# Split merge-gate products, probabilities turned one step later and paired roots in a two-layer attention, recurrence and expert kernel

## The reference

```
(sh1, sc1, g1, sh2, sc2, g2) = silu(cond) @ w_ada + b_ada         # two conditions: context, latent
h = rmsnorm(x) * (1 + sc1) + sh1
q, k, v, xr, gr, ga, gb = split(h @ w_in)                         # gr, ga, gb: 1024 columns each
att = softmax(q k / sqrt(128), with a sink) v                      # 8 heads x 3 blocks of 128 queries
xc  = conv4(xr)
for d in (forward, backward):                                      # 8 channel blocks of 128 each
    r, i = sigmoid(blockdiag(xc) + b)                              # two gates
    log_a = -8 * r * softplus(-lambda);  a = exp(log_a)
    h = a * h + sqrt(1 - a^2) * (i * xc)                           # a scan over time
rnn = sum of both directions
merged = sigmoid(ga) * (att @ w_ap) + sigmoid(gb) * ((gelu(gr) * rnn) @ w_rp)
x = x + g1 * (merged @ w_out)
x = x + g2 * experts(rmsnorm(x) * (1 + sc2) + sh2)                 # 16 experts, top 2
```

## Time and profile before

| | |
|---|---|
| median of 3 runs | 1539.71 us (1538.92 to 1546.27) |
| the profiled execution | 1542.47 us, of which the span is 1540.7 us |
| mean granted TensorE clock | 0.992 of full speed |
| busy share of the span | PE 97%, PEld 78%, DVE 72%, ACT 60%, POOL 12% |
| gate steps of layer 0 | 204 to 333 us |
| gate steps of layer 1 | 953 to 1081 us |
| experts | about 480 to 775 us and 1223 to 1517 us |

### The profile page before, as it was taken

One profiled execution on the slowest core, in us unless ns is written; L12 is line 12 of the kernel. 1 busy time (PEld: TensorE's weight loads), 2 busy tenths in 40 slices (PEclk: granted clock), 3 DMA queues, 4 the chain that ended last, 5 costly groups with the idle time before them and its releaser, 6 DMA issues.

```text
span 1540.7 us, 19726 instructions
## 1 busy us (share of the span) xinstructions
PE 1490.0 (97%) x7489; PEld 1197.9 (78%) x7489; DVE 1108.2 (72%) x1719; ACT 922.4 (60%) x1178; POOL 181.7 (12%) x220
## 2 busy tenths in 40 slices
PE   6999999999999999999999999999999999999996
PEld 4699876669986888888768998666899678888885
DVE  4447656674647999999864665767564689999986
ACT  1323569981225877778752245899422478778774
POOL 0100012210121000000230000222004111000002
PEclk8999999999999999999999999999999999999999
DMA  9455432216539999999854554111431899999993
GB/s 353 168 188 202 163 115 82 99 59 216 203 144 340 362 401 408 410 406 409 311 186 174 187 196 165 63 64 62 163 111 55 312 358 408 413 411 408 405 354 124
DMA packets 132421, 371.98 MB, mean 241 GB/s; under 512 B 9184, under 2 KB 12640, under 8 KB 132320
## 3 DMA queue, kind: packets, MB, share of 16 engines
q1 hardware_dynamic: 113728, 326.57, 56.4%
q0 software_dynamic: 10144, 24.13, 4.5%
q10 hardware_dynamic: 8448, 19.94, 3.3%
HBM read 350.66 MB, written 19.94 MB: 241 GB/s over the span
## 4 chain that ended last, share of the span: by engine, by line
PE 86%; DVE 6%; ACT 4%; DMA 2%; issue 2%; SPq 0%; DVEq 0%; ACTq 0%
PE bank L561 24%; PE bank L917 23%; PE bank L923 12%; PE bank L550 10%; PE bank L571 3%; PE bank L768 2%; DMA ring<-in_w_ada 2%; PE bank L889 2%; PE bank L741 1%; PE bank L596 1%; PE bank L580 1%; PE bank L678 1%; PE bank L673 1%; PE bank L960 1%; PE bank L1025 1%
## 5 line engine op out<-in xcount | busy, mean ns | idle before, releaser
L1977 DVE TENSOR_TENSOR spot_low<-spot,piece_high 128x2048 fp32r<-128x2048 f32 x192 | 433.6, 2286 | 33.2 <-ACT piece_high L1336 32.0
L1336 ACT ACTIVATE piece_high<-spot 128x2048 fp32r<-128x2048 f32 x192 | 366.7, 1917 | 44.5 <-PE bank L923 42.4
L917 PE MATMUL bank<-piece_high,ga_r 128*128 128x512 f32 x768 | 308.7, 402 | 2.9 <-DVE spot_low L1977 1.6
L917 PE MATMUL bank<-spot_low,ga_r 128*128 128x512 f32 x768 | 301.7, 393 | 0.0
L923 PE MATMUL bank<-piece_high,ga_r 128*128 128x512 f32 x768 | 210.9, 396 | 3.3 <-DVE ga_r L1983 3.3
L561 PE MATMUL bank<-parts_r,ga_r 128*128 128x384 f32 x768 | 202.6, 345 | 0.0
L550 PE MATMUL bank<-hT,ring 128*128 128x384 f32 x544 | 184.7, 494 | 4.1 <-ACT ga L1274 2.3
L923 PEld LDWEIGHTS bank<-piece_high,ga_r 128*128 128x128 f32 x768 | 144.0, 188 | 38.6 <-DVE ga_r L1983 4.4
L917 PEld LDWEIGHTS bank<-piece_high,ga_r 128*128 128x128 f32 x768 | 144.3, 188 | 36.1 <-DVE spot_low L1977 2.4
L917 PEld LDWEIGHTS bank<-spot_low,ga_r 128*128 128x128 f32 x768 | 144.6, 188 | 30.6
L550 PEld LDWEIGHTS bank<-hT,ring 128*128 128x128 f32 x544 | 102.0, 192 | 70.8 <-issue 3.6
(11 more groups left out here) (336 smaller groups left out, 2333.3 us busy)
## 6 DMA issues: line engine op xcount, KB each, us to landing
spot<-in_w_gate_up SPq DMA_DIRECT2D x128, 1024.0 KB, 8.0
spot<-in_w_down SPq DMA_DIRECT2D x64, 1024.0 KB, 8.0
ring<-in_w_ada SPq DMA_DIRECT2D x24, 2048.0 KB, 9.0
ring<-in_w_in SPq DMA_DIRECT2D x22, 2048.0 KB, 7.9
expert_rows<-gb ACTq DMA_DIRECT2D x28, 512.0 KB, 7.0
ring<-in_w_attn_proj SPq DMA_DIRECT2D x4, 2048.0 KB, 8.1
ring<-in_w_rnn_proj SPq DMA_DIRECT2D x4, 2048.0 KB, 12.4
ring<-in_w_out SPq DMA_DIRECT2D x4, 2048.0 KB, 8.6
```

What stands on the lines that cost most here:

```text
L917: pe.matmul(out[n], high[:, 2 * q + k, :], w[:, k, n * 512:(n + 1) * 512], start=(q == 0 and k == 0 and i == 0), stop=False)
L1336: ac.activation(highs[p % HIGHS], spots[u], ACT.Copy).then_inc(S("piece_high"), 1)
L1977: ve.tensor_tensor(spots_low[u], spots[u], highs[p % HIGHS].bitcast(F32), ALU.subtract)\
```

## The change

1. ga and gb become split products. Their high parts (16 per layer) are made by POOL, in its queue between the gate-weight DMAs; their low parts by DVE. High parts lie in the buffers G0 to G2 (tile gb), spare, and X0, X1 (tile xc, once the scans of pairs 0 to 5, or 0 to 11, have ended).
2. `probs_turned(i - 1)` stands after `scores(i)` and ahead of product i, where `probs_turned(i)` stood after it; `pt_copy` and `att_copy` follow by a step, `pt` has one buffer instead of two.
3. The recurrent temporaries have three sets. `scan` follows two steps after its pair's gates. The square goes: where sqrt(1 - a^2) was the root of (1 + a^2) * tanh(x), with a = exp(-x), it is now (1 + a) times the root of tanh(x/2). So the root comes first, straight from `lru_tables`, and DVE multiplies after it.
4. `lru_root` runs for two pairs in even steps, instead of one in each.
5. The rnn tiles are split in high and low during the ap products (`rnn_split`), pairs 14 and 15 are scanned there, the split attention output and merged go to hT and qT instead of parts.
6. `mod_sum` turns the four 128x128 blocks with transposes, and DVE adds the four groups out of PSUM with one reduction and adds the bias in a second operation.

The diff, cut to its core:

```diff
-SPLIT = [(kind, n) for kind in ("q", "xr", "gr", "ap", "rp", "wo") for n in range(KT)]
+SPLIT = [(kind, n) for kind in ("q", "xr", "gr", "ga", "gb", "ap", "rp", "wo") for n in range(KT)]
+LATE = 5 * KT
+HIGH_HOMES = (["G0", "G1", "G2"] * 2 + ["G0", "G1"]
+              + ["G2", "spare", "X0", "G2", "spare", "X0", "spare", "X1"]
+              + ["X0", "spare", "X1"] + (["A0", "A1", "A2", "spare"] * KT)[:3 * KT - 3])
+SCANS_OF_HOME = {"X0": 6, "X1": 12}
...
                 for j in range(4):
-                    mm = pe.matmul(bank[:, 2 * j:2 * j + 2], ada_part(cc)[:, j * P:(j + 1) * P], sumsel,
-                                   start=(j == 0), stop=(j == 3), skip_group_check=True)
+                    mm = pe.transpose(bank[:, j * P:(j + 1) * P], ada_part(cc)[:, j * P:(j + 1) * P], ident)
...
                     scores(i)
-                    if kind == "gr":
-                        split_product(l, kind, i, parts_r[:, 0], parts_r[:, 1])
-                    else:
-                        product((l, kind, i % KT), s, i % 4, h_all)
+                    if i >= 1:
+                        probs_turned(i - 1)
+                    split_product(l, kind, i % KT, parts_r[:, 0], parts_r[:, 1])
                     if i % 4 == 0 and i <= KT:
                         mod_sum(l, 7 + i // 4)
-                    probs_turned(i)
...
                     ac.activation(th, a, ACT.Tanh, bias=c_log[1], scale=c_log[1])
-                    link(ac.activation(a, a, ACT.Exp, bias=c_log[0], scale=c_log[0]))
-                    if m:
-                        ac.wait_ge(S("lru_square"), m)
-                    ac.activation(a2, a, ACT.Square).then_inc(S("lru_act"), 1)
+                    ac.activation(a, a, ACT.Exp, bias=c_log[0], scale=c_log[0]).then_inc(S("lru_act"), 1)
...
                 for i in range(3 * KT):
+                    if i > KT:
+                        lru_tables(i - KT - 1)
                     exps(i)
-                    if i > KT:
-                        lru_root(i - KT - 1)
+                    if i >= 1:
+                        pt_copy(i - 1)
+                    if i >= 2:
+                        att_copy(i - 2)
+                    if i > KT and i % 2 == 0:
+                        lru_root(i - KT - 2)
+                        lru_root(i - KT - 1)
...
-                ve.tensor_tensor(modT[:, cc * 4:cc * 4 + 4, 0], pair[:, :, 0], b, ALU.add)
-                ve.tensor_tensor(modT[:, cc * 4:cc * 4 + 4, 1], pair[:, :, 1], b, ALU.add)\
+                link(ve.tensor_reduce(m, groups, AX.X, ALU.add))
+                ve.tensor_tensor(m, m, b.rearrange("p (j a) -> p j a", a=1).broadcast_to([P, 4, 2]), ALU.add)\
...
+                def scan_inputs(n):
+                    ve.wait_ge(S("lru_act"), m + 1)
+                    ve.scalar_tensor_tensor(ti, ti, 1.0, xc[:, j, :], ALU.add, ALU.mult)
+                    ve.wait_ge(S("root_ready"), m + 1)
+                    link(ve.scalar_tensor_tensor(th, a, 1.0, th, ALU.add, ALU.mult))
+                    link(ve.tensor_tensor(th, th, ti, ALU.mult))
...
                     softmax_max(i)
+                    if i > KT + 1 and i % 2:
+                        scan_inputs(i - KT - 2)
+                    if i >= KT and i % 2 == 0:
+                        low_part(2 * KT + i + 1)
                     softmax_norm(i)
...
-                    if i > KT:
-                        one_minus_square(i - KT - 1)
-                        scan(i - KT - 1)
+                    if i >= KT - 1 and i % 2:
+                        low_part(2 * KT + i + 1)
+                    if i > KT + 1:
+                        if i % 2 == 0:
+                            scan_inputs(i - KT - 2)
+                        scan(i - KT - 2)
...
                 for n in range(KT):
-                    low_part(EARLY + n + AHEAD)
+                    low_part(LATE + n + AHEAD)
+                    if n < 2:
+                        scan_inputs(14 + n)
+                        scan(14 + n)
+                    for j in RNN_SPLIT_AT.get(n, ()):
+                        rnn_split(j)
...
+                def high_part(at):
+                    kind, n = SPLIT[at]
+                    s, use, _ = CHUNK_SLOT[CHUNK_AT[(l, f"{kind}{n // 4}")]]
+                    po.wait_ge(S(f"w_loaded{s}"), 16 * (use + 1))
+                    if home_user_ahead(at):
+                        po.wait_ge(S("gemm_done"), G_AT[(l, *SPLIT[home_user_ahead(at)])] + 1)
+                    elif HIGH_HOMES[at - EARLY] in SCANS_OF_HOME:
+                        po.wait_ge(S("lru_used"), l * 16 + SCANS_OF_HOME[HIGH_HOMES[at - EARLY]])
+                    else:
+                        po.wait_ge(S("gemm_done"), G_AT[(l, *SPLIT[at - PAIRS_OF_PARTS])] + 1)
+                    po.tensor_copy(w_high_part(kind, n), slot_kn(s)[:, :, n % 4 * P:(n % 4 + 1) * P])\
+                        .then_inc(S("w_high_p"), 1)
+                for n in range(2):
+                    gate_weights(n)
+                    high_part(EARLY + n)
+                for n in range(2 * KT - 2):
+                    if n:
+                        gate_weights(n + 1)
+                    high_part(EARLY + 2 + n)
+                gate_weights(15)
```

More of the change, by code:

```diff
@@ L113, with home_user_ahead @@
 PAIRS_OF_PARTS = 3
-LATE_HIGHS = 4
+LATE = 5 * KT
[3 more added lines that the diff above has]
+SCANS_OF_HOME = {"X0": 6, "X1": 12}
+def home_user_ahead(at):
+    same = [b for b in range(EARLY, at) if HIGH_HOMES[b - EARLY] == HIGH_HOMES[at - EARLY]]
+    return same[-1] if same else None
 UNITS = [(h, b) for h in range(HEADS) for b in range(3)]
+RNN_SPLIT_AT = {2: (0,), 3: (1, 2), 4: (3,), 5: (4, 5), 6: (6,), 7: (7,)}
 PAIRS = [(d, j) for j in range(KT) for d in range(2)]
@@ L307, in build @@
         w_parts = [(part(gaf_r, i), part(gbf_r, i)) for i in range(PAIRS_OF_PARTS)]
-        late_high = [part(spare_r, 0)] + [part(hTf, i) for i in range(LATE_HIGHS - 1)]
+        high_home = {"spare": part(spare_r, 0)}
+        for i in range(3):
+            high_home[f"G{i}"], high_home[f"A{i}"] = part(gbf_r, i), part(flat_parts_r, i)
+        for i in range(2):
+            high_home[f"X{i}"] = part(xcf, i)
         ring_r = sb_r("ring")
@@ L771, in _ @@
                         attend(i - 1)
+                probs_turned(3 * KT - 1)
                 modulation(l, 10)
@@ L1289, in scaled @@
                         .then_inc(S("router_a"), 1)
-                for at in range(EARLY, len(SPLIT)):
-                    if at + AHEAD < len(SPLIT):
+                for at in range(LATE, len(SPLIT)):
+                    if LATE < at < len(SPLIT) - AHEAD:
                         high_part(at + AHEAD)
@@ L1666, in _ @@
                         mod_add(l, 4)
+                if l:
+                    link(ve.memset(xp[:, 2 + CTX:2 + LAT0], 0.0))
                 for j in range(KT):
```

116 lines of the change are left out of this document (57 added, 59 removed).

## The result

| | median us | lowest to highest | runs |
|---|---|---|---|
| before | 1540.90 | 1538.92 to 1546.27 | 4 |
| changed | 1523.41 | 1520.51 to 1526.79 | 4 |

The ratio is 0.9879, with an interval of 0.9854 to 0.9904: 17.5 us faster, where 31 were forecast. The profiled execution took 1526.79 us with a span of 1524.8; it is the slowest of the four and 3.4 us above their median.

A forecast was written before the change was run, and what follows sets the result against it. PE bounded the kernel, and DVE would bound the changed gate steps. Gates -21, gr -2, mod_sums -7 and tail -1 sum to -31 us: 1542.47 to 1511.5 profiled, 1509 as median; range 1488 to 1545.

The forecast's parts named there:

- port rival: Gate steps: a cast of about 1.05 us wholly on DVE's path, full step 8.1 us; 1522 to 1546 us, chance 0.23.
- my own sign: Gate steps: PE idle before split products or scores ended by DVE confirms DVE as bound; ended by ACT's tanh, uneven roots.
- The sign for the port: Gate steps: DVE's low part at 1.22 us would refute the port cost, at 1.5 or more confirm it.
- The products and the sum without the port: Gate steps: split products 4.23 us instead of 5.16; DVE's 6.75 plus root wait 0.3, before the port's 0.3.
- port term: Gate steps: POOL's cast holds up DVE operations with two SBUF inputs, 0.54 x 0.6 = 0.3 us per step.
- "whole cast" rival: Gate steps: a 1.05 us cast wholly on DVE's path; step 8.1 us, about 1528 to 1532; span 1522 to 1546, chance 0.23.
- slower rival: Full gate steps: POOL wins the port with a slow cast, 2.4 us per step; about 1569 us, chance 0.10.
- gr term: gr steps: transposes of the probabilities turned one step later get a product more of cover; -1 us per layer, -2.
- The mod_sum: Modulation sums by transposes: 0.5 us less each, 16 of 24 on PE's path; -7 us taken.
- The root's wait: Even gate steps: DVE waits 0.6 us for ACT's root, 0.3 per step; bounds 0 and 0.9 per even step.
- The tail: Between the loop and ap: of PE's 1.0 us idle, -0.5 us per layer, -1 in all.
- The rnn splits and scans in ap: ap products: some 30 us of DVE beside 34 of PE costs nothing; without cover, 2 to 4 us per layer.

The follow-up runs named there:

- e3: Against the changed kernel: ACT takes the two roots of even gate steps ahead of the exponentials instead of behind them; 1526.3 us.
- e1: Against the changed kernel: POOL writes zeros into the high parts of ga and gb instead of casting weights, so it reads nothing; 1508.3 us.
- e5: Against the changed kernel: the 16 casts per layer move from POOL to ACT, two in each odd step ahead of the tanh; 1519.3 us.
- e8: e5 and e6 together: casts on ACT, and copies ahead of the exponentials; 1507.6 us.
- e2: Against the changed kernel: each POOL cast for ga and gb is done twice, one after the other; 1546.6 us.
- e7: Against the changed kernel: the modulation sums are products against the 0/1 matrix again instead of transposes and a reduction; 1531.4 us.
- e10: Against the changed kernel: one root in each step from the tenth on instead of two in every second step; 1558.0 us.
- e9: Against e8: the last merge-gate cast on ACT moves from the end of step 21 to behind the exponentials of step 22; 1502.8 us.
- e4: Against the changed kernel: ga and gb products in f32 again, without casts and low parts, right operand the high part of h alone; 1529.1 us.
- e6: Against the changed kernel: ACT copies pt and the attention output ahead of the exponentials in all 24 steps; 1513.3 us.
- e11: The edits of e1 and e6 together on the changed kernel: zeros stored instead of casts, and copies ahead of the exponentials; 1500.8 us.

## Why the prediction was right and wrong

**Right in direction and range, too high in the gain.** 1523 lies 14 us above the 1509 forecast, 1 us outside the likeliest case's own span (1500 to 1522) and just inside that of the port rival (1522 to 1546). Of the 15 us between forecast and profile, 8.6 lie in the gate steps and tail, 6.7 in the gr steps and 2.5 in the mod_sums; ap and what lies outside the layers gave 2.5 back. That the time stayed in the range with two terms this far off owes something to luck.

**The signs.** The products took 4.2 us and the table loads in the gate steps of layer 0 fell from 28 to 14, as named. PE's long idles there ended with ACT's tanh, which by my own sign "would put it on the uneven roots". e3 moved the roots and gained nothing, and e1 left the roots alone and took half of the idle away, so that sign did not tell the two apart: the tanh comes last in a chain that DVE's stretches push later. What is left of the idle in e1, 4.9 and 4.6 us with the tail's 1.4, may be the roots'; no run shows it. The sign for the port was badly chosen as well: 28 of the 32 low parts kept 1.22 us, one took 1.39 and three over 2, while most of the stretches fell on other operations.

**The products and the sum without the port: right.** The split product took 4.23 us. Without the port term my sum gives 14 x 7.05 + 2 x 6.9 + 1 = 113.5 us per layer against 128.9, which with the tail's 0.5 puts the gate stage at 133.7 - 15.9 = 117.8. With no read on POOL it was 118.5 and 118.4. One part of that sum did not come: the last cast, for which I took 1 us of wait, ran at 310.65 us and its low part at 313.31 us, with no wait on it. On ACT, in e5 and e8, the same cast did hold up the list.

**The port term was mis-sized.** I took 0.3 us per step: a stretch of 0.54 us for 60% of the casts, 8.4 us in all. The share was about right: 18 of the 32 casts met a stretched operation. The stretch itself was taken at half its size: it measured 1.0 us on average and up to 1.5. The rows I scaled from were of other POOL operations and of one collision. The stretches add up to 8 us in layer 0 and 10.8 in layer 1, and e1 puts what reaches the gate stage at 6.7 and 10.0 us, 0.52 us per cast; e2 has 0.62. That is 8 us more than I took, nearly all that is missing in the gate steps. Some 6 us of the 16.7 come through the four stretches at half clock, about 1.5 us each, a path that no term foresaw. The 1.05 us taken for the cast itself was right (1.055). My "whole cast" rival priced a step at 1.05 and came too high, since 14 of the 32 casts met no operation that they stretched. The slower rival had its threshold at 1.36 us per step; the cast kept its length beside DVE, as that rival had it, but with 1.06 us the threshold could not be reached. e2, with two casts per step, did end slower than before, by 0.3%.

**The gr term had the wrong sign.** "Turned one step later these have a whole product more of cover: -1 us per layer" looked at the transposes and left out the copy behind them on ACT, which stands behind the exponentials and their wait for DVE. The stage got 2.4 us longer per layer; with the copy moved it got 1.6 shorter than before, somewhat more than forecast.

**The mod_sum: right in kind, too large.** 0.36 us instead of 0.5 on PE's path, and of the 16 some have no share in it (rp in layer 1 did not move). The stages show 4.5 us for the forecast 7; undoing it (e7) cost 4.6 in the stages.

**The root's wait: right, slightly high.** 0.6 us per even step was forecast, 2.4 us over seven was measured in layer 0, 0.34 each. I did not see how much hung on the pairing, with DVE's list written as it is: e10 is 35 us slower.

**The tail: wrong sign, small.** I took -0.5 us per layer; the idle ahead of ap went from 1.02 to 1.41 us in both layers. It now ends with DVE's split of the last attention output, behind the copy that still stands after `lru_tables(15)` on ACT.

**The rnn splits and scans in ap:** right in the main. ap takes 37.2 us as before in layer 0 and 1.2 less in layer 1; ahead of the first rp product of layer 0 PE waits 1.11 us for an rnn split. The gate products wait for no gate weights, so the casts ahead of these on POOL cost nothing there.

## What to carry to other kernels

When work is moved to POOL, expect each of its SBUF reads to stretch the DVE operation with two SBUF inputs that it meets, here by about the cast's own length; a write-only operation cost DVE nothing in e1, and the same casts on ACT came within 2 us of no casts, though they made ACT the busier of the two (100.4 us against DVE's 95.7 in the gate steps of e9). When a step is delayed by one iteration, follow all its instructions on all engines: the consumer's copy belongs ahead of this iteration's waits, in the time in which its engine is idle. And where two engines feed each other inside a step, what counts is what stands in a list ahead of the awaited result: asking for a fresh result only in every second step can be worth more than the instructions it saves.

## What the runs showed of the hardware that I had not expected

- Four stretches of 3.4 us at half clock (granted clock 0.50, the lower level of 1.2 GHz) in the gate steps, each beside a PE idle of over 2 us. In layer 0 they began 0.7 and 1.2 us after the ends of the idles of 2.18 and 2.19 us, in layer 1 beside idles of 2.39 and 2.27 us; an idle of 2.60 us in layer 1 had none. The profiled executions of the kernel before, e1, e4, e6, e9 and e11 have none there, though e6 has an idle of 2.57 us in each layer, and e5 has an idle of 2.41 us in each layer and a stretch only in layer 1. e2 has seven. So a wait of PE can, but need not, cost most of its length a second time.
- The DVE operation was stretched also where it had begun before the cast: the scan at 258.43 us ran 0.64 us before the cast of 259.07 began and ended 0.55 us after it, so it was stretched by more than the cast's length. The Trainium skill (SBUF — State Buffer, Who interferes with whom) has it that issue order decides who blocks; these rows do not show DVE keeping the ports, and in e2 both sides paid. Which of the two yields, and when, stays open.
